# Two-layer hybrid trunk: another order of the pairs' products, conv's blocks as z, b, u, c, and other due times for side work

## What is computed

```python
h = rms_norm(x, pre_g)
proj = h @ w_in                      # 2048 x 24576: 12 sections of 1536, 3 gates of 2048
o_a = dilated_mixture_attn(q_a, k_a, v_a) * silu(z_a)
o_c = b_c * causal_short_conv(c_c * u_c, conv_w, conv_b) * silu(z_c)
o_r = retention(q_r, k_r, v_r) * silu(z_r)
merged = (sigmoid(g_a) * (o_a @ w_branch_a) + sigmoid(g_c) * (o_c @ w_branch_c)
          + sigmoid(g_r) * (o_r @ w_branch_r))
x = x + rms_norm(merged @ w_out, post_g)
```

## Time and profile before

| what | us |
|---|---|
| median of 3 runs | 2733.85 (2733.63 to 2734.94) |
| the profiled execution's own time | 2733.36 |
| span of that execution in the trace | 2731.5 |
| PE busy | 2706.8 (99% of the span) |
| DVE busy | 1890.0 (69%) |
| ACT busy | 1304.1 (48%) |
| chain that ended last: PE, DVE, ACT | 92%, 5%, 1% of the span |

### The profile page before, as it was taken

How to read it: one execution, slowest core, us unless ns; L and a number is a source line. 1 busy time by engine, 2 the same in 40 slices (tenths; PEclk the granted TensorE clock), 3 DMA queues, 4 the chain that set the end, 5 groups by cost and what they waited for, 6 DMA issues and landing times.

```text
span 2731.5 us, 30218 instructions
## 1 busy us (share of the span) xinstructions
PE 2706.8 (99%) x12120; PEld 2239.9 (82%) x12120; DVE 1890.0 (69%) x2102; ACT 1304.1 (48%) x1504; POOL 29.3 (1%) x42
## 2 busy tenths in 40 slices
PE   9999999999999999999999999999999999999998
PEld 7888888888888888888878888888888888888887
DVE  6656764888775666678576667658887656666784
ACT  6554554555453344454454545445555433444543
POOL 0000000000000000000000000000000000000000
PEclk9999999999999999999999999999999999999999
DMA  9667465665665676656576774656656666766563
GB/s 332 215 218 233 164 224 196 228 206 197 210 231 191 216 233 209 218 203 222 180 236 202 223 232 154 233 183 234 221 181 211 235 196 209 238 213 218 201 217 122
DMA packets 299291, 579.43 MB, mean 212 GB/s; under 512 B 12304, under 2 KB 37264, under 8 KB 298896
## 3 DMA queue, kind: packets, MB, share of 16 engines
q1 hardware_dynamic: 260976, 517.50, 56.6%
q10 hardware_dynamic: 37168, 55.13, 6.8%
q0 software_dynamic: 1008, 4.87, 0.6%
HBM read 548.10 MB, written 29.36 MB: 211 GB/s over the span
## 4 chain that ended last, share of the span: by engine, by line
PE 92%; DVE 5%; ACT 1%; issue 1%; DMA 1%; POOL 0%; ACTq 0%; SPq 0%; DVEq 0%; POOLq 0%
PE ps L912 28%; PE ps L913 28%; PE ps L914 28%; DVE w_trail L1253 2%; PE ps L878 2%; PE ps L879 2%; PE ps L877 2%; DVE raw L1263 1%; ACT w_lead L986 1%; DMA bounce_z<-z_sb 0%; PE ps L823 0%; PE ps L821 0%; PE ps L820 0%; PE ps L799 0%; PE ps L803 0%
## 5 line engine op out<-in xcount | busy, mean ns | idle before, releaser
L1253 DVE TENSOR_TENSOR w_trail<-raw,w_lead 128x1024 fp32r<-128x1024 f32 x1045 | 1269.1, 1223 | 788.1 <-ACT w_lead L986 784.9
L986 ACT ACTIVATE w_lead<-raw 128x1024 fp32r<-128x1024 f32 x1045 | 1098.5, 1059 | 1292.9 <-PE ps L914 1130.1
L912 PE MATMUL ps<-w_lead,hT_lead 128*128 128x512 f32 x2944 | 1152.7, 392 | 14.9 <-DVE w_trail L1253 13.6
L914 PE MATMUL ps<-w_lead,hT_trail 128*128 128x512 f32 x2944 | 1146.2, 389 | 0.0
L913 PE MATMUL ps<-w_trail,hT_lead 128*128 128x512 f32 x2944 | 1146.1, 389 | 0.0
L912 PEld LDWEIGHTS ps<-w_lead,hT_lead 128*128 128x128 f32 x2944 | 552.9, 188 | 140.0 <-DVE w_trail L1253 23.5
L914 PEld LDWEIGHTS ps<-w_lead,hT_trail 128*128 128x128 f32 x2944 | 552.9, 188 | 115.3
L913 PEld LDWEIGHTS ps<-w_trail,hT_lead 128*128 128x128 f32 x2944 | 553.1, 188 | 112.9
L912 PE MATMUL ps<-w_lead,oT_lead 128*128 128x512 f32 x576 | 224.2, 389 | 0.0
L914 PE MATMUL ps<-w_lead,oT_trail 128*128 128x512 f32 x576 | 224.1, 389 | 0.0
L913 PE MATMUL ps<-w_trail,oT_lead 128*128 128x512 f32 x576 | 224.1, 389 | 0.0
(11 more groups left out here) (130 smaller groups left out, 1158.9 us busy)
## 6 DMA issues: line engine op xcount, KB each, us to landing
raw<-w_in SPq DMA_DIRECT2D x381, 1024.0 KB, 5.3
raw<-w_out SPq DMA_DIRECT2D x32, 1024.0 KB, 5.1
raw<-w_branch_a SPq DMA_DIRECT2D x24, 1024.0 KB, 5.7
raw<-w_branch_c SPq DMA_DIRECT2D x24, 1024.0 KB, 5.3
raw<-w_branch_r SPq DMA_DIRECT2D x24, 1024.0 KB, 5.5
bounce_q<-vq_sb ACTq DMA_DIRECT2D x18, 512.0 KB, 3.5
vq_sb<-bounce_q ACTq DMA_DIRECT2D x72, 128.0 KB, 4.1
bounce_z<-z_sb ACTq DMA_DIRECT2D x18, 512.0 KB, 2.9
```

The costliest lines, as they stand in the source:

```text
L912: pe.matmul(acc, lead[:, k, tok(t)], wl, start=opens, stop=False)
L914: last = pe.matmul(acc, trail[:, k, tok(t)], wl, start=False, stop=closes)
L986: act.activation(w_lead[:, (l * HALVES + h) % SPLIT_SLOTS, :], raw[:, SLOT_OF[l, i][0], part:part + HALF * COLS], ACT.Copy).then_inc(lead_ ...
L1253: dve.tensor_tensor(w_trail[:, s, :], raw[:, SLOT_OF[l, i][0], part:part + HALF * COLS], w_lead[:, s, :].bitcast(F32), ALU.subtract).then_ ...
```

## The change

The order of the pair's seven products and of its chunk loads changes, and with it the places of the four sums (`SUMS` names for each sum the step of `PAIR_ORDER` behind whose first or second T it stands, and the product whose split must be done before). The kinds of the 22 units stay as they were. Conv's blocks come in the order z, b, u, c. Due times of conv's `gate`, `z` trip and later steps and of attention's last `z_back`, `z` and `out` change. The rest makes the helpers follow (`closes` marks the last matmul into a bank).

```diff
-ROLES = {"attention": "vqkz", "conv": "bzuc", "retention": "vqkz"}
+ROLES = {"attention": "vqkz", "conv": "zbuc", "retention": "vqkz"}
...
-PAIR_ORDER = ("p1", 0, "q5", 0, "p6", 0, "p7", 0, "q3", 1, "p2", 1, "q4", 1, 1)
-PAIR_CHUNK_ORDER = ((0, 0), (1, 0), (0, 2), (1, 1), (0, 3), (1, 2), (0, 1), (1, 3))
-
-SUM_AFTER = {"q5": "p1", "p6": "q5", "p7": "p6", "q4": "p2"}
+PAIR_ORDER = ("p1", 0, "q3", 0, "q5", 0, "p2", 0, "p6", 1, "p7", 1, "q4", 1, 1)
+PAIR_CHUNK_ORDER = ((0, 0), (0, 2), (1, 0), (1, 1), (0, 3), (0, 1), (1, 2), (1, 3))
+
+
+SUMS = {"q5": (1, "p1"), "p7": (3, None), "p6": (5, "q5"), "q4": (9, "p6")}
+
+
+
+P2_LAST = PAIR_ORDER.index("p2") > max(i for i, step in enumerate(PAIR_ORDER) if step == 0)
...
+def sum_unit(kind, n):
+
+
+    step = PAIR_ORDER[SUMS[kind][0]]
+    if step in PRODUCTS:
+        return UNIT_AT[step, n, CHUNK // HALF - 1]
+    before = sum(s == step for s in PAIR_ORDER[:SUMS[kind][0]])
+    return UNIT_AT["half", n + step, 2 * CHUNK + HALF * before]
...
-            kind, n, at = place(l, h)
-            if kind in PRODUCTS and PRODUCTS[kind][1] is not None and at == 0:
+        for n in PAIRS:
+            for kind in SUMS:
                 i, c = PRODUCTS[kind][1]
-                uses[l, CHUNK_LIST.index((n + i, c))] = h
+                at = l, CHUNK_LIST.index((n + i, c))
+                uses[at] = max(uses.get(at, 0), sum_unit(kind, n) + 1)
...
     "attention": [("q_away", 2 * B - 1), ("q_back", 2 * B + 1), ("k_away", 3 * B - 1), ("k_back", 3 * B + 1),
-                  ("exp", 4 * B + 1), ("z_away", 5 * B + 4), ("z_back", 5 * B + 6), ("out", 6 * B + 1)],
-    "conv": [("z_away", 2 * B + 1), ("z_back", 2 * B + 3), ("prod_away", 4 * B), ("prod_back", 4 * B + 2),
-             ("out", 5 * B)],
+                  ("exp", 4 * B + 1), ("z_away", 5 * B + 4), ("z_back", 6 * B + 4), ("out", 6 * B + 6.5)],
+    "conv": [("z_away", 2 * B + 10.5), ("z_back", 2 * B + 13.5), ("prod_away", 2 * B + 15), ("prod_back", 2 * B + 17),
+             ("out", 2 * B + 23)],
...
-                 + pieces("probs", 4 * B + 3) + [("values", 5 * B + 3), ("z", 6 * B), ("out", 6 * B + 2)],
-    "conv": [("gate", 2 * B), ("z", 2 * B + 6), ("prod", 4 * B + 5), ("conv0", 4 * B + 5), ("conv1", 4 * B + 6),
-             ("conv2", 4 * B + 7), ("product", 5 * B), ("out", 5 * B + 1)],
+                 + pieces("probs", 4 * B + 3) + [("values", 5 * B + 3), ("z", 6 * B + 6), ("out", 6 * B + 7)],
+    "conv": [("gate", 2 * B + 10), ("z", 2 * B + 17), ("prod", 2 * B + 20), ("conv0", 2 * B + 20), ("conv1", 2 * B + 21),
+             ("conv2", 2 * B + 22), ("product", 2 * B + 23), ("out", 2 * B + 24)],
...
-SUM_DUE = {UNIT_AT[before, n, 1]: (kind, n) for n in PAIRS for kind, before in SUM_AFTER.items()}
+SUM_DUE = {sum_unit(kind, n): (kind, n) for n in PAIRS for kind in SUMS}
...
-                    closes = k == CHUNK - 1 and what != "q3"
+                    closes = k == CHUNK - 1 and (what == "p2" and P2_LAST or what not in ("q3", "p2"))
...
-                        closes = k == BLOCKS[n][2] - 1 and (n not in PAIR_OF or begun)
+                        closes = k == BLOCKS[n][2] - 1 and (n not in PAIR_OF or begun or t == 0 and not P2_LAST)
...
-                elif what in SUM_AFTER and part == 0:
-                    act.wait_ge(summed, len(SUM_AFTER) * pair_no(l, n) + list(SUM_AFTER).index(what) + 1)
+                elif what in SUMS and part == 0:
+                    act.wait_ge(summed, len(SUMS) * pair_no(l, n) + list(SUMS).index(what) + 1)
...
-                dve.wait_ge(*split_done(l, UNIT_AT[SUM_AFTER[what], n, CHUNK // HALF - 1]))
+                if SUMS[what][1] is not None:
+                    dve.wait_ge(*split_done(l, UNIT_AT[SUMS[what][1], n, CHUNK // HALF - 1]))
```

## The result

The changed kernel takes 2713.15 us (median of 4 runs, 2712.87 to 2713.52) where the kernel before takes 2734.39 (4 runs, 2733.63 to 2735.46): ratio 0.9922 with a 95% interval of 0.9906 to 0.9937. It is 21.2 us faster. Of this, 20.5 us lie between the two profiled executions (2733.36 and 2712.87 us); the rest is the scatter of the runs around them.

What follows compares the result with a forecast made beforehand. PE, busy 99% of the span, bounds the kernel; only its waits can be won. -19.8 + 1.2 = -18.6 us from 2733.36 gives 2714.8, plus 0.49 for the median 2715.2; own range 2713.5 to 2717.2, 8 in 10 to 2722.

Steps and rivals of the forecast that it cites:

- T of unit 9 was to have 1.1 us in hand: Conv's pairs: T of unit 9 runs from 13.85 to 15.07, needed by 16.20, so 1.1 us early.
- 0.12 after that T has ended: Conv's pair before the change: PE starts unit 5 at 9.62, 1.46 late and 0.12 us after its T ended.
- the pairs hold 2 x 2.9 + 2 x 0.5 + 2 x 1.1 + 6 x 1.8 = 19.8 us of waiting: All pairs of two layers, one row for each kind: 19.8 us of PE waiting, the most the change can win.
- The low end of the range: Whole kernel: 2713.5 us, with all 19.8 us of waiting gone and half a us of spread.
- conv's term: Conv's pairs (u and c): six pairs, each 1.8 us too long, taken from one row.
- The second term: Attention gates' two pairs: z parts beside the load cost 0.6 us each, 1.2 us in all; bounds 0 and 1.6 each.
- the rule alone: Attention gates' two pairs: DMA engines taking turns between queues make the load lose the parts' whole share, 3.2 us, 2717.2.
- The signs to look for: Pairs: 153 matmuls in 34.7 to 34.9 us (attention up to 36), PE's T waits about 5, ACT's sum waits near nothing.
- if ACT waits for loads of raw inside pairs: Inside pairs: ACT waiting for loads of raw would show the forecast wrong; no size given.
- (1): Only the due times act, not the order; conv gates' and retention gates' pairs keep 3.2 us: 2718.4; chance 0.1.
- (2): T of unit 15 late as chunk (1, 2) lands after 7.7: 1.4 us per pair, 2723 (half) or 2731 (all); chance 0.12.
- (3): Before unit 9: chunk (0, 1) lands after 9.5 us and starves PE, 2739.4 and above; chance 0.04.

## Why the prediction was off by two microseconds

**The mechanism held, to 0.1 us.** For conv's pair it gave, from the pair's start, T of unit 2 at -1.40, the sum for q5 at -0.26, T of units 3, 4 and 5 at 1.95, 3.45 and 4.87, sums at 6.01 and 11.64, T of unit 9 at 13.85; measured are -1.36, -0.22, 1.98, 3.46, 4.89, 6.03, 11.64 and 13.84. The loads were to land by 11.5 and 20.4 and were in at 11.36 and 20.32. b's two copies take the 1.25 us that z's two sigmoids took. T of unit 9 was to have 1.1 us in hand; one more T showed 1.2. The difference is a reading: the prediction lets PE start "0.12 after that T has ended", but in the pair of before T of unit 5 starts at 8.35, takes 1.22 and ends at 9.57, 0.05 ahead of PE's 9.62, so each of its "needed by" times is 0.07 too early. (Its 26.1 for T of unit 15 in conv's pair is that T's end; it starts at 24.9 there, and at 24.76 by the trace.)

**What failed is the step "the pairs hold 2 x 2.9 + 2 x 0.5 + 2 x 1.1 + 6 x 1.8 = 19.8 us of waiting. That is the most this change can win".** The twelve pairs of before, measured one by one from first matmul to the next unit, hold 2.89 and 2.87 (attention), 0.55 twice, 1.12 and 1.10 (retention), and 1.90, 1.89, 1.89, 1.89, 1.99 and 1.91 (conv): 20.6. 0.7 of the missing 0.75 us lies in conv's term, 6 x 1.8 = 10.8 for 11.5, since one row, its starts rounded to 0.1 us, stood for six pairs. An upper bound that is a product of a rounded row and a count is no bound to a tenth. The low end of the range, 2713.5, was built on it.

**The second term, 1.2 us for the attention gates' pair, measured nothing.** Its step was "so I take 0.5 and a start of 0.1 behind a wait": the load was to land 0.5 us later for the parts beside it, and PE to pay for it. The load took 5.0 us, and T of unit 16 started at 26.98 where 27.2 stood. Its lower bound, 0 each, was right, and the low end of the range allowed for it; the price of 0.5 was a share of the earlier trace rows that the place did not show. The other place, half a step later, has it: 2.5 us in two pairs by the experiment, where the rule alone was put at 3.2.

Term by term: 1.2 for attention, 0.7 for the pairs, and 0.2 because the median stood 0.28 above the profiled execution instead of 0.49: 2715.2 - 2.1 = 2713.1. The range failed because its low end took the sum's own terms as known and gave half a us for everything else. Half a us is also less than the scatter: the first pair, ahead of which every kernel here does the same matmuls, starts anywhere from 327.69 to 328.87 us in the twelve traces, and one of the changed kernel's four runs, at 2713.52, lies inside the range.

**The signs to look for.** 34.7 us for the 153 matmuls in all pairs, PE's waits for T nearly gone (one left where about 5 were foreseen), ACT's wait for sums gone, T of unit 5 ending 6.1 us after the start: right. But the text also said the forecast would be wrong "if ACT waits for loads of raw inside pairs", and ACT does, 38.4 us in 24 waits. That sign was badly chosen, against the prediction's own sum: with the load in at 11.5 and L of unit 9 free to start at 12.8, ACT was bound to wait for it and PE was not. Only a wait of PE's tells.

**The rivals.** (1) fell: the order alone brings 13.3 us. (2) did not occur: the load takes 5.0 to 5.3 us in all twelve pairs. A wait before unit 15 does appear when T of unit 9 comes 1.25 us later, but by a later issue of the load, not by a longer landing. (3) did not occur, but its mechanism and its feedback were shown by the later load.

No kernel tried is faster than the changed one beyond the scatter; the pairs are at 40.8 us each, the time of their 180 matmuls.

## What to carry to other kernels

Where short and long units alternate on the engine that sets the time, count for each the latest moment its operands may come, and put long side work of the feeding engine where a long unit follows; a later sum is only good if other splits lie between it and its use. Ask of every delay which buffer it frees late: the load behind it makes the next unit late too. And sum a bound over all instances rather than from one rounded row of each kind.

## What the runs showed of the hardware beyond this

Conv's z parts at their new place, in the plain stretch after the pair and beside loads that take 8.8 to 11.2 us there, need far longer than the 3.1 us that was the median of all z parts before. The changed kernel, the parts of layer 1's first conv block (issue durations, first and last start; landing):

```profile
L1113 ACTq DMA_DIRECT2D z_sb<-bounce_z x4: 309/452/454, 1869.7 to 1871.0; - x4
...
DMA to landing us min/median/max: 6.0/7.1/9.2
```

7.1 us here, 2.8 for attention's in the same kernel, for the same 128 KB. That the loads beside them are the reason was not tried by itself. It costs PE nothing, since the turn that reads them is due late too, but without room to spare: the last part lands at 1880.18 us, and the turn starts at 1880.27. The prediction had costed the move by its issues alone.
